# Last projection of a hybrid S5 / short-convolution / mixture-of-experts network: load order, one weight's low part, routing batches and banks changed at its two ends

## The reference

```python
b_g, c_g, v = jnp.split(h @ w_in, 3, axis=-1)
z = conv(c_g * v)                        # width 3, causal, per channel
x = x + (1 + g1) * ((b_g * z) @ w_out)   # "last projection"
hn = rmsnorm(x, norm2_g) * (1 + sc2) + sh2
g = softmax(hn @ wg + bg); best group; two best of its 8 experts   # routing
y[token] += weight * expert(hn[token])   # 32 experts, two per token
```

## Time and profile before

| | us |
|---|---|
| median of 3 runs (lowest, highest) | 6134.78 (6132.90, 6139.69) |
| the profiled execution's own time | 6134.56 |
| its span | 6132.8 |
| phase cout | 4202.6 to 4636.8 |
| TensorE matmul busy, whole span | 5823.3 (95%) |
| VectorE / ScalarE / GpSimd busy | 3881.5 (63%) / 2218.6 (36%) / 2205.8 (36%) |

### The profile page before, as it was taken

How to read it: one execution, slowest core, us unless ns; L and a number is a source line. 1 busy time by engine, 2 the same in 40 slices (tenths; PEclk the granted TensorE clock), 3 DMA queues, 4 the chain that set the end, 5 groups by cost and what they waited for, 6 DMA issues and landing times. The chain is left out here.

```text
span 6132.8 us, 83088 instructions
## 1 busy us (share of the span) xinstructions
PE 5823.3 (95%) x28082; PEld 4748.1 (77%) x28083; DVE 3881.5 (63%) x5502; ACT 2218.6 (36%) x3316; POOL 2205.8 (36%) x2123
## 2 busy tenths in 40 slices
PE   7999989999889999999989999998997999999994
PEld 5876668888768888888868888886775888888884
DVE  5889955554445544555536588888995454556555
ACT  2334432222234433434425333323333333444434
POOL 6555538870022322323224433340112222222222
PEclk9999989999999999999989999999997999999997
DMA  4565664442167667767647666665545656777767
GB/s 153 170 191 156 188 226 151 141 136 83 66 225 222 196 182 209 215 193 221 190 128 275 246 201 216 224 201 194 169 152 191 195 157 193 210 216 243 211 199 283
DMA packets 630211, 1168.18 MB, mean 190 GB/s; under 512 B 126052, under 2 KB 222884, under 8 KB 629001
## 3 DMA queue, kind: packets, MB, share of 16 engines
q1 hardware_dynamic: 427600, 803.93, 38.8%
q0 software_dynamic: 97744, 326.67, 19.7%
q10 hardware_dynamic: 104682, 35.19, 2.2%
HBM read 870.66 MB, written 294.67 MB: 190 GB/s over the span
## 5 line engine op out<-in xcount | busy, mean ns | idle before, releaser
L2790 DVE SCALAR_TENSOR_TENSOR m_o<-m_pO,m_weight_of,m_gate 128x512 f32<-128x512 f32 x316 | 234.1, 747 | 713.4 <-POOLq L2435 382.8
L2757 DVE TENSOR_TENSOR m_w_lo<-m_w_raw,m_w_hi 128x1024 fp32r<-128x1024 f32 x512 | 596.4, 1216 | 0.1
L2417 POOL COPY m_gather_now<-m_gather_of 128x1 int32 (+1 forms) x161 | 180.1, 1119 | 1155.1 <-DMA x<-m_o,m_scatter_now 911.2
L2588 ACT ACTIVATE m_xT_hi<-m_pX 128x512 fp32r<-128x512 f32 x320 | 191.4, 599 | 998.8 <-PE m_pB L145 994.3
L143 PE MATMUL m_pA<-m_w_lo,m_xT_hi 128*128 128x512 f32 x1280 | 517.5, 404 | 16.5 <-DVE m_xT_lo L2768 16.5
L2576 ACT ACTIVATE m_w_hi<-m_w_raw 128x1024 fp32r<-128x1024 f32 x512 | 505.6, 1053 | 50.2 <-DMA m_w_raw<-in_moe_w_dram 28.8
L2529 PE MATMUL m_pO<-m_w_lo,m_hT_hi 128*128 128x512 f32 x1280 | 513.8, 401 | 0.5 <-ACT m_hT_hi L2593 0.5
L145 PE MATMUL m_pA<-m_w_hi,m_xT_hi 128*128 128x512 f32 x1280 | 503.1, 393 | 0.0
L144 PE MATMUL m_pA<-m_w_hi,m_xT_lo 128*128 128x512 f32 x1280 | 500.5, 391 | 0.0
L2529 PE MATMUL m_pO<-m_w_hi,m_hT_hi 128*128 128x512 f32 x1280 | 499.6, 390 | 0.0
L143 PE MATMUL m_pB<-m_w_lo,m_xT_hi 128*128 128x512 f32 x1280 | 498.1, 389 | 0.0
(11 more groups left out here) (552 smaller groups left out, 13718.7 us busy)
## 6 DMA issues: line engine op xcount, KB each, us to landing
m_w_raw<-in_moe_w_dram SPq DMA_DIRECT2D x384, 1024.0 KB, 7.5
conv_op_raw<-xr SPq DMA_DIRECT2D x84, 1024.0 KB, 5.6
glu_ada<-in_ada_w_dram POOLq DMA_DIRECT2D x96, 256.0 KB, 3.3
a_x<-in_x_dram SPq DMA_DIRECT2D x32, 512.0 KB, 3.6
a_ada<-in_ada_w_dram POOLq DMA_DIRECT2D x64, 256.0 KB, 3.5
s_u<-u SPq DMA_DIRECT2D x64, 256.0 KB, 2.7
s_r<-k SPq DMA_DIRECT2D x64, 256.0 KB
glu_x<-in_x_dram SPq DMA_DIRECT2D x32, 512.0 KB, 5.1
```

Source lines behind the costliest of these rows:

```text
L2417: pool.tensor_copy(gx[:], gidx[:, bass.ds(t, 1)]).then_inc(gi_ready, 1)
L2588: act.activation(xT_hi[:, 4 * q:4 * q + 4, :], pX[:, 4 * q:4 * q + 4, :], ACT.Copy).then_inc(xt_hi, 1)
L2757: tt(W13[s][1][:, m, k:k + 2, :], W13[s][0][:, m, k:k + 2, :], W13[s][2][:, m, k:k + 2, :].bitcast(F32), ALU.subtract).then_inc(w13_lo, 1)
L2790: dve.scalar_tensor_tensor(out=ob[:, n, :], in0=pO[:, n, :], scalar=wslot[:, bass.ds(tile_, 1)], in1=gate2[:, n, :], op0=ALU.mult, op1=ALU ...
```

## The change

Four edits.

1. Loads at the start of cout: SP now issues source tile 3, weight 5, x of tile 1, source tile 2, x of tile 0, then waits for the last stores of z (`z_last`, now shared by both phases), and then issues the seven small loads. ScalarE in conv no longer waits for its two stores.
2. The low part of weight 3 is made by VectorE in cout, between `left_sums(0, 3)` and `low(0, 3)`, instead of by GpSimd at the end of conv; product 3 of pair 0 waits for it.
3. Routing batches of layer 1 are (0, 3), (3, 4), ... (27, 4), (31, 1). `choose` moves from step 3 to the end of step 1 of odd p, that is ahead of `from_bank` of product 1 and of the reading of the logits of tile 2p-3 in step 2. Batch 6 is settled in step 3 of the last pair (before: step 5) and placed after the pairs. The last batch has 2 record DMAs in place of 4, batch 7 has 8 in place of 4.
4. Tile 30's transposes, router product and sum use banks 1 and 2, and its copies have buffers of their own; the ranks of the last three batches use bank 0. The order after the pairs changes: `odd_done` ahead of both norms, ScalarE's square of tile 31 ahead of the copy of tile 29, TensorE's ranks of batch 7 behind tile 31.

```diff
+    SHIFTED = [(0, 3)] + [(t, 4) for t in range(3, NT - 1, 4)] + [(NT - 1, 1)]
...
+        late_banks = banks[:, 1:3, :].rearrange("p a (k f) -> p (a k) f", f=P)
+        pH_of = lambda n: late_banks if n == NT - 2 else pH_[:]
+        ranks_in = lambda b: bank[0][...] if b >= LAST - 2 else pH_[:, 4, ...]
...
+            odd_rows(1)
             sp.dma_start(w_raw[5][:], ...).then_inc(w_ld, 16)
             x_odd(0)
-            odd_rows(1)
+            even_rows(1)
             x_even(0)
+            sp.wait_ge(z_last, 32)
             sp.dma_start(gain[:], ...)
...
-            even_rows(1)
...
             def slot(p, s):            # VectorE
                 elif s == 1:
                     if p:
                         normed(p - 1, 1)
+                    if chosen_at(p) is not None:
+                        choose(chosen_at(p))
                 elif s == 3:
-                    if chosen_at(p) is not None:
-                        choose(chosen_at(p))
-                    elif placed_at(p) is not None:
+                    if placed_at(p) is not None:
                         settle(placed_at(p))
...
             left_sums(0, 3)
+            w_low(3)
             low(0, 3)
...
+            odd_done(PAIRS - 1)
             normed(PAIRS - 1, 0)
-            odd_done(PAIRS - 1)
             normed(PAIRS - 1, 1)
-            out_logits(2 * (PAIRS - 2) + 1)
+            out_logits(NT - 3)
+            place(LAST - 2)
+            out_logits(NT - 2)
             choose(LAST - 1)
             settle(LAST - 1)
-            out_logits(2 * (PAIRS - 1))
             place(LAST - 1)
-            out_logits(2 * (PAIRS - 1) + 1)
+            out_logits(NT - 1)
             choose(LAST)
...
             router_halves(NT - 3)      # TensorE
+            turned_hn(NT - 2)
             router_sum(NT - 3)
-            turned_hn(NT - 2)
             router_halves(NT - 2)
             router_sum(NT - 2)
-            batch_ranks(LAST - 1)
             turned_hn(NT - 1)
             router_halves(NT - 1)
             router_sum(NT - 1)
+            batch_ranks(LAST - 1)
             batch_ranks(LAST)
...
-            act.wait_ge(z_last, 32)    # end of conv
+            act.wait_ge(n_w_hi, BY_VECTOR + 1)
...
-            pool.wait_ge(n_w_hi, BY_VECTOR + 1)
-            pool.tensor_tensor(ahead.w_lo[BY_VECTOR][:], ahead.w_raw[BY_VECTOR][:], ...)
-            pool.wait_ge(n_w_last, 1)
```

More of the change, by code:

```diff
@@ L1247, in __init__ @@
         self.columns = lambda b: [k * self.B + j for k in range(2) for j in range(self.BATCHES[b][1])]
+        self.shifted_columns = lambda b: [k * self.B + j for k in range(2) for j in range(self.SHIFTED[b][1])]
         self.token, self.base = core.sb(ctx, "route_token", [P, 2, self.B]), core.sb(ctx, "route_base", [P, NE])
@@ L1716, in project_out @@
     r_rec, r_st = sem("route_records"), sem("route_records_stored", 2)
-    LAST = len(routes.BATCHES) - 1
-    records_of = lambda b: 16 * sum(len(routes.columns(c)) for c in range(b % 2, b + 1, 2))
+    LAST = len(routes.SHIFTED) - 1
+    records_of = lambda b: 16 * sum(len(routes.shifted_columns(c)) for c in range(b % 2, b + 1, 2))
     ODD_ROW, EVEN_ROW = (0, 1, 2, 3, 6), (4, 5)
@@ L1951, in from_bank @@
                 dve.wait_ge(prod, m + 1)
-                return tt(out, bank[m % BANKS][:], other, ALU.add).then_inc(read, 1)
+                return tt(out, bank[m % BANKS], other, ALU.add).then_inc(read, 1)
             def normed(p, s):
@@ L2020, in slot @@
                         out_logits(2 * (p - 1))
-                    if placed_at(p) is not None:
+                    if placed_at(p) is not None and more:
                         place(placed_at(p))
@@ L2150, in _ @@
                     slot(p, s)
-            out_h(2 * (PAIRS - 2) + 1)
             square(PAIRS - 1, 1)
-            out_lT(2 * (PAIRS - 2) + 1)
-            for n in range(NT - 2, NT):
+            for n in range(NT - 3, NT):
                 out_h(n)
@@ L2170, in op @@
                     pe.wait_ge(left_lo, m - 1)
[L2171 to L2172 removed]
+                if p == 0 and r >= 3:
+                    pe.wait_ge(w_lo_ready, r - 2)
                 if m >= BANKS:
@@ L2175, in op @@
                 for k in range(KH):
-                    last = product(pe, bank[m % BANKS][:], (hi[r][:, k, :], lo[r][:, k, :]), (w_hi[r][:, k, :], w_lo[r][:, k, :]),
+                    last = product(pe, bank[m % BANKS], (hi[r][:, k, :], lo[r][:, k, :]), (w_hi[r][:, k, :], w_lo[r][:, k, :]),
                                    k == 0, k == KH - 1)
@@ L2181, in turned_hn @@
                 pe.wait_ge(hn_ready, n + 1)
-                if n:
-                    pe.wait_ge(lg_out, n)
-                if n % 2 and n < NT - 1 and placed_at((n + 1) // 2) is not None:
+                if n and n != NT - 2:
+                    pe.wait_ge(lg_out, n - (1 if n == NT - 1 else 0))
+                if n % 2 and n < NT - 3 and placed_at((n + 1) // 2) is not None:
                     pe.wait_ge(r_out, placed_at((n + 1) // 2) + 1)
-                if n == NT - 1:
-                    pe.wait_ge(r_out, LAST)
+                if n == NT - 2:
+                    pe.wait_ge(read, 7 * (PAIRS - 1) + 6)
                 for k in range(KD):
-                    last = pe.transpose(pH[:, k, :], hn[n % 2][:, k * P:(k + 1) * P], ident[:])
+                    last = pe.transpose(pH_of(n)[:, k, :], hn[n % 2][:, k * P:(k + 1) * P], ident[:])
                 last.then_inc(ht_psum, 1)
@@ L2193, in batch_ranks @@
                 pe.wait_ge(r_mask, b + 1)
-                m = routes.BATCHES[b][1]
-                out = pH[:, 4, 0:m * NE]
+                if b == LAST - 2:
+                    pe.wait_ge(read, 7 * (PAIRS - 1) + 3)
+                elif b > LAST - 2:
+                    pe.wait_ge(r_out, b)
+                m, out = routes.SHIFTED[b][1], ranks_in(b)
                 pe.matmul(out, upper[:], tmp[:, 0:m, :].rearrange("p t e -> p (t e)"), start=True, stop=False)
@@ L2203, in router_halves @@
                     at_ = 64 * (k % 2)
-                    last = pe.matmul(pH[at_:at_ + NL, 1, :], wr[:, k, :], hT[:, k, :], start=k < 2, stop=k >= KD - 2)
+                    last = pe.matmul(pH_of(n)[at_:at_ + NL, 1, :], wr[:, k, :], hT_of(n)[:, k, :], start=k < 2, stop=k >= KD - 2)
                 last.then_inc(lt_psum, 1)
@@ L2211, in router_sum @@
                 pe.wait_ge(lt_out, n + 1)
-                pe.matmul(pH[:, 0, 0:NL], lT[0:64 + NL, :], select[0:64 + NL, :], start=True, stop=True).then_inc(lg_psum, 1)
+                pe.matmul(pH_of(n)[:, 0, 0:NL], lT_of(n)[0:64 + NL, :], select[0:64 + NL, :], start=True, stop=True).then_inc(lg_psum, 1)
             for p in range(PAIRS):
```

53 lines of the change are left out of this document (28 added, 25 removed).

## The result

| | before | changed | ratio, 95% interval |
|---|---|---|---|
| median, us (17 runs each) | 6136.10 | 6147.96 | 1.0018 [1.0012, 1.0025] |
| profiled execution's span, us | 6132.8 | 6147.8 | |

The forecast of 6148 holds, and the sign with it. The ratio's median lies just inside the 0.2% that I had taken as the limit of "no change", so by the median the outcome "slower by over 0.2%", which had 0.53, was missed by a hair; the interval covers both. That the total is right is luck in part: the pairs cost 3.7 us less than I said, the start gained some more, the end costs 2.2 more, and the median before is now 1.3 us above the one that I had added the sum to.

A forecast was written before the change was run, and what follows sets the result against it. Bound: in the pairs TensorE and VectorE are tied, so a new idle microsecond of VectorE costs one. -4.2 - 2.0 - 4.75 + 23.3 + 0.8 = +13.15 on 6134.56 gave 6147.7, stated as 6148; range 6135 to 6155.

The forecast's parts named there:

- slower by over 0.2%: Outcome for the whole kernel: slower by more than 0.2%, 12.3 us, with the line at 6147.0 us; chance 0.53.
- hand-over (lock and store wait): End of conv: VectorE's 4.98 us instruction falls to 0.75 (4.2 us gained), and the store wait goes (2.0 us gained).
- start of cout: Cout's start: VectorE gets 4.75 us earlier, its 7.05 us idle less 2.29 us for weight 3's low part.
- pairs: stalls, five: Pairs 5, 7, 9, 11, 13: transposes wait 3.35 us for the logits, and VectorE idles 2.3 us in each.
- pairs: slow stretches: Behind that wait in pairs 5 to 13 TensorE's clock falls, costing 1.85 us in each odd pair.
- pair 3: Pair 3, not yet tied: wait of about 1.7 us plus 0.85 for half a chance of slow clock, 2.55 us.
- end: After the pairs: eight record DMAs delay the next phase, which then issues fewer; between -0.45 and +2.1 us, taken as +0.8.
- cover: Odd pairs: how much later product 5 may come before VectorE misses it, 0.8 us.
- The first rival: Odd pairs, product 5: VectorE swallows the wait ahead of the transposes, middle costs 0 to 1 us; 6125 us, chance 0.10.
- The second: Pairs: the clock stays up over the waits, middle 13.2 us, total +3.05; 6138 us, chance 0.13.
- lands 2.2 us later [...] Plus 1.1: End of cout: last record DMA, issued at 4636.7, lands 2.2 us later; the next phase starts 1.1 us after that.
- The fourth rival: End of conv and start of cout: first edits fail their purpose, half the 10.95 us gain is lost; 6153 us, chance 0.07.

The follow-up runs named there:

- start_only: Kernel before with only the new load order and store wait, and weight 3's low part on VectorE: 6126.39 us, ratio 0.9983.
- filled: Changed kernel with 13 unread products on TensorE ahead of the even tile's transposes in odd pairs 5 to 13: 6143.62 us, ratio 1.0011.
- ring_choose_behind: Changed kernel with eight places for logits instead of four, and `choose` behind the reading of the logits again: 6129.60 us, ratio 0.9989.
- half_choose: `ring_choose_behind` with the first 6 of `choose`'s 13 instructions ahead of the reading of the logits, the other 7 behind: 6132.71 us, ratio 0.9996.
- late_wait: Changed kernel with GpSimd's wait for the landed records moved into the next phase, behind its own two: 6146.03 us, ratio 1.0017.
- start_and_banks: `start_only` plus tile 30's banks, last ranks in bank 0 and the last product ahead of the norms, old batches: 6127.89 us, ratio 0.9990.
- start_and_banks2: `start_and_banks` with batch 7's ranks moved between the transposes and router product of tile 31 on TensorE: 6121.70 us, ratio 0.9974.

## Why the prediction was right, and where not

| term | predicted | measured | from |
|---|---|---|---|
| hand-over (lock and store wait) | -6.2 | -5.87 | idle of TensorE; alone -4.21 and -1.62 |
| start of cout | -4.75 | -4.99 | router product of tile 0; `start_only` -4.98 |
| from there to tile 1's transposes | no term | -0.86 | goes with the execution |
| pairs: stalls, five | 11.5 | 11.8 | rest of the 19.64; `filled` less `ring_choose_behind`: 2.3 each |
| pairs: slow stretches | 9.25 (5 of 1.85) | 6.3 (4 of 1.57) | stages view; changed less `filled` 6.0 |
| pair 3 | 2.55 | 1.56 | distance of the transposes |
| end | +0.8 | +3.0 | distance to the first expert product |
| sum | 13.15 | 10.9 | medians 11.86 |

- The mechanism in the pairs was right step by step: place, wait (3.35 predicted, 3.43 measured), cover, stall, clock. The first rival (VectorE swallows the wait) needed a cover of 5 us; `half_choose` measured 0.84. The second (the clock stays up) was true of one pair in five.
- The mis-sized terms are the slow stretch and its number. I took the clock as certain behind 3.35 us. In two kernels with ten such waits (changed, `late_wait`) it fell behind seven. In pair 3 I gave half a chance to a slow stretch; none came.
- The other mis-sized term is the end. The step that failed is "lands 2.2 us later [...] Plus 1.1": from the last record DMA to the next phase it was 8.43 us, not 3.3. The 2.2 was misread. The view of the earlier trace rows mixes layers: the short landings are those of layer 0's records (L1385), the 7.6 is a fetch out of the buffer (L2408), and for the 60 record DMAs of the phase in question (L1837) the trace pairs no landing at all. But for the eight that the two expert phases issue and wait for (L2404), it does. Views by line, kernel before:

```profile
L1385 POOL DMA_INDIRECT slots<-route_record,route_place x60: 954/958/1607, 1084.3 to 1672.7; - x60
...
DMA to landing us min/median/max: 2.1/2.1/5.5
```

```profile
L2404 POOL DMA_INDIRECT slots<-route_record,route_place x8: 954/968/993, 1687.0 to 4642.6; - x8
...
DMA to landing us min/median/max: 5.3/5.9/6.4
```

With the median of this row, 5.9, in place of 2.2 the forecast of the next phase's start would have been 3.7 us later, of the 5.1 that this step was short. The other 1.4 stays open, and why the same instruction lands after 2.1 us in one stretch and after 5.3 to 6.4 in another no run shows. VectorE's part came 2.4 us earlier than I had it (GpSimd's first DMA of batch 7 stood 31.8 us behind the transposes of tile 28, forecast 34.2): the norm of tile 30 ended 1.2 us earlier, and its router product took 1.07 us, at full clock, and not 1.9. So the error in the beginning of the next phase was 2.8 and not 5.1. The late landing stood in the bounds (7.6, "+5"), though its 7.6 came from another DMA.
- The fourth rival (early edits do not do what they are for) is excluded by the three kernels that carry them alone.
- The rule of the Trainium skill ("TensorE: Matmul & The Clock Gate", section "Loop structure matters more than you think") gave 6138, as I had applied it. But the example there has the next matmuls follow immediately, and in this place they wait for 3.4 us, so it speaks of another case. Behind the wait of 3.43 us the granted clock was 0.63 once and 1.00 once, and work in the wait (`filled`) kept it at 1.00 and took 6 us from the pairs. Behind the waits of 1.41 and 1.54 us the trace agrees.

## What to carry to other kernels

When two engines are tied, the order inside one engine's list decides: put what another engine waits for first, and give it one more buffer if the reuse of a buffer is what forces the other order (18.4 us here for 576 bytes per partition). Price a new wait as its length less the cover, plus a chance of a slow clock stretch. And when a change shortens a chain, look for what had been hidden behind it: at a phase's end, indirect DMAs issued last became the bound. Take the time to landing from the same instructions in the same stretch, not from a view that mixes stretches (2.1 against 5.3 to 6.4 us here). The best kernel keeps the two early edits, the old batches and `choose` in its old place, and adds the banks for tile 30 with the ranks moved up: 6121.70, 14.9 us under the kernel before beside it (6136.60), 26 under the changed one.

## What the runs showed of the hardware

- The clock's fall is not decided by the length of a wait alone: 3.43 us came both with it and without, in one trace, ahead of the same instructions. A wait of 3.29 to 3.45 us brought it in seven cases of ten.
- 13 products laid into such a wait kept the granted clock at 1.00 in all five places (`filled`).
- From the issue of a phase's last record DMA to GpSimd's first instruction of the next phase 8.26 to 8.44 us pass in six kernels with the explicit wait (changed, `filled`, `ring_choose_behind`, `half_choose`, `start_and_banks`, `start_and_banks2`), and 7.06 in `late_wait` without it. The Trainium skill puts a small DMA of this path at about 2.0 us ("DMA: Bandwidth & Descriptors", section "Anatomy of one DMA — SWDGE (gpsimd) path"); the 2.1 us of layer 0's records agree, the 5.3 to 6.4 us of the same form at the start of the expert phases do not.
